# The round count of an expert loop moved from VectorE to GpSimd, and three VectorE instructions reordered in front of the loop

## What is computed

```python
g_logits = z @ w_group + b_group            # 4 groups, the best one is taken
e_logits = z @ w_router + b_router          # 8 experts in each group
top_p, top_i = lax.top_k(softmax(e_in_group), 2)
combine = sum(one_hot(global_idx, 32) * top_w[..., None]) * g_p
for e in range(32):
    gate, up = jnp.split(z @ w_gate_up[e], 2, axis=-1)
    y = y + combine[..., e:e + 1] * ((silu(gate) * up) @ w_down[e])
return rms_norm(x + y, final_norm_g)
```

## Time and profile before

| what | us |
|---|---|
| median of 3 runs | 868.09 |
| lowest and highest run | 867.6, 868.18 |
| span of the profiled execution, first to last instruction | 867.1 |
| start of the first expert step (half 0 on TensorE) | 390.99 |

### The profile page before, as it was taken

How to read it: one execution, slowest core, us unless ns; L and a number is a source line. 1 busy time by engine, 2 the same in 40 slices (tenths; PEclk the granted TensorE clock), 3 DMA queues, 4 the chain that set the end, 5 groups by cost and what they waited for, 6 DMA issues and landing times.

```text
span 867.1 us, 14585 instructions
## 1 busy us (share of the span) xinstructions
PE 852.8 (98%) x5738; PEld 753.9 (87%) x5738; DVE 789.1 (91%) x785; ACT 648.9 (75%) x631; POOL 22.2 (3%) x30
## 2 busy tenths in 40 slices
PE   8999999999999999999999999999999999999996
PEld 6999999999889999877788888888888888888874
DVE  6458999999977787789999999999999999999996
ACT  6563424344554466587999999999999999999996
POOL 0110000000000000016000000000000000000000
PEclk9999999999999999999999999999999999999999
DMA  9952555445452449646999999999999999999971
GB/s 354 425 223 98 193 193 194 178 158 177 169 194 98 144 173 410 248 166 237 392 426 423 429 426 431 428 427 431 427 430 426 430 429 427 430 427 430 426 313 49
DMA packets 20743, 270.70 MB, mean 312 GB/s; under 512 B 2272, under 2 KB 2528, under 8 KB 4448
## 3 DMA queue, kind: packets, MB, share of 16 engines
q1 hardware_dynamic: 20144, 268.33, 75.9%
q10 hardware_dynamic: 560, 1.84, 0.5%
HBM read 269.10 MB, written 1.05 MB: 312 GB/s over the span
## 4 chain that ended last, share of the span: by engine, by line
PE 84%; DVE 13%; issue 2%; ACT 1%; DMA 0%; DVEq 0%; ACTq 0%
PE ps L1598 24%; PE ps L1612 12%; PE ps L1412 9%; PE ps L1414 9%; PE ps L1413 9%; PE ps L1583 4%; PE ps L1622 3%; DVE lo L1117 3%; DVE lo L842 2%; DVE conv L941 2%; PE ps L1429 2%; PE ps L1427 2%; PE ps L1428 2%; PE ps L1696 2%; PE ps L1703 1%
## 5 line engine op out<-in xcount | busy, mean ns | idle before, releaser
L1117 DVE TENSOR_TENSOR lo<-raw,hi 128x2048 fp32r<-128x2048 f32 x142 | 319.1, 2283 | 0.3 <-ACT hi L655 0.3
L655 ACT ACTIVATE hi<-raw 128x2048 fp32r<-128x2048 f32 x141 | 264.9, 1916 | 15.7 <-PE ps L1598 15.7
L444 ACT ACTIVATE hi<-raw 128x2048 fp32r<-128x2048 f32 x62 | 118.6, 1914 | 57.6 <-PE ps L1414 37.6
L842 DVE TENSOR_TENSOR lo<-raw,hi 128x2048 fp32r<-128x2048 f32 x61 | 139.2, 2286 | 20.4 <-ACT hi L444 19.0
L1412 PE MATMUL ps<-inA,hi 128*128 128x256 f32 x544 | 155.0, 285 | 1.4 <-DVE lo L842 1.4
L1598 PE MATMUL ps<-hi,xeT 128*128 128x512 f32 x384 | 154.5, 402 | 0.1
L1414 PE MATMUL ps<-inA,lo 128*128 128x256 f32 x544 | 153.9, 283 | 0.0
L1413 PE MATMUL ps<-inA,hi 128*128 128x256 f32 x544 | 153.9, 283 | 0.0
L1598 PE MATMUL ps<-lo,xeT 128*128 128x512 f32 x384 | 150.2, 391 | 0.0
L1117 DVE TENSOR_TENSOR lo_last<-raw,hi_last 128x2048 fp32r<-128x2048 f32 x48 | 109.6, 2283 | 0.0
L1412 PEld LDWEIGHTS ps<-inA,hi 128*128 128x128 f32 x544 | 104.4, 192 | 2.4 <-DVE lo L842 2.4
(11 more groups left out here) (258 smaller groups left out, 1293.1 us busy)
## 6 DMA issues: line engine op xcount, KB each, us to landing
raw<-in_w_experts SPq DMA_DIRECT2D x96, 2048.0 KB, 13.2
raw<-in_w_dense SPq DMA_DIRECT2D x28, 2048.0 KB, 7.8
raw<-in_w_dense SPq DMA_DIRECT2D x3, 1024.0 KB, 12.6
x_sb<-in_x SPq DMA_DIRECT2D x2, 512.0 KB, 3.6
raw<-in_w_dense SPq DMA_DIRECT2D x2, 512.0 KB, 8.3
mem_sb<-in_mem SPq DMA_DIRECT2D x1, 1024.0 KB, 16.3
x_again<-in_x ACTq DMA_DIRECT2D x1, 1024.0 KB, 17.3
out<-x SPq DMA_DIRECT2D x3, 256.0 KB, 2.1
```

The source lines that it names most:

```text
L444: return nc.scalar.activation(conv_half(hi, N), raw_half(slot, h), ACT.Copy)
L655: nc.scalar.activation(expert_half(hi, N0), raw_flat(slot, k % 2), ACT.Copy).then_inc(hi_made, 1)
L842: nc.vector.tensor_tensor(conv_half(lo, N), raw_half(slot, h), conv_half(hi, N).bitcast(f32), ALU.subtract).then_inc(lo_made, 1)
L1117: nc.vector.tensor_tensor(expert_half(lo, N0), raw_flat(expert_slot(m), k % 2), expert_half(hi, N0).bitcast(f32), ALU.subtract).then_inc(l ...
```

## The change

VectorE keeps the maximum and signals `most_counted` with it. GpSimd compares it and writes `loops`, behind the weights' split and ahead of L423. On VectorE, the low part of half 2 moves ahead of the third piece, `make_pick(1)` and the maximum stand behind the third piece and ahead of the low part of half 3. The waits of the first step on TensorE and ScalarE go to `most_counted`; TensorE waits for `loops_made` before it loads the counts.

```diff
--- before.py
+++ after.py
@@ -219,6 +219,7 @@
         route_for_exp, route_exp, member_made, ranked, rank_made = map(
             sem, ("route_for_exp", "route_exp", "member_made", "ranked", "rank_made"))
         loops_made, comb_made = sem("loops_made"), sem("comb_made")
+        most_counted = sem("most_counted")
         first_again = sem("first_again")
         pick_made, put_made, gathered, xeT_hi, xeT_made = map(sem, ("pick_made", "put_made", "gathered", "xeT_hi", "xeT_made"))
         gate_out, up_out, slotted, slot_sums_made = map(sem, ("gate_out", "up_out", "slotted", "slot_sums_made"))
@@ -419,6 +420,15 @@
             pool_link(nc.gpsimd.tensor_tensor(weight, weight, R["tmp"], ALU.add))
             pool_link(nc.gpsimd.tensor_tensor(total, weight[:, :, 0:PAIRS], weight[:, :, PAIRS:E], ALU.add))
             three_parts(total, lambda k: comb[:, :, :, k], comb_made)
+
+            most, more_turns, further = stat[:, 12:13], stat[:, 13:14], stat[:, 14:15]
+            pool.wait_ge(most_counted, 1)
+            pool_link(nc.gpsimd.tensor_scalar(more_turns, most, float(SLOTS), float(TURNS), ALU.is_gt, ALU.mult))
+            for r in range(2, MAX_ROUNDS):
+                pool_link(nc.gpsimd.tensor_scalar(further, most, float(SLOTS * r), float(TURNS), ALU.is_gt, ALU.mult))
+                pool_link(nc.gpsimd.tensor_tensor(more_turns, more_turns, further, ALU.add))
+            nc.gpsimd.tensor_scalar(loops[:, 1:2], more_turns, float(TURNS - 2), None, ALU.add)
+            nc.gpsimd.tensor_scalar(loops[:, 0:1], more_turns, float(TURNS - 1), None, ALU.add).then_inc(loops_made, 1)
             for r in range(1, MAX_ROUNDS + 1):
                 ins = nc.gpsimd.tensor_scalar(rank_tab[:, :, r * PAIRS:(r + 1) * PAIRS, :], rank_tab[:, :, 0:PAIRS, :],
                                               -float(SLOTS * r), None, ALU.add)
@@ -743,7 +753,7 @@
                 nc.scalar.activation(gu_sb[:, 0:FF], G0, ACT.Copy).then_inc(gate_out, 1)
                 if start:
                     act.wait_ge(comb_made, 2)
-                    act.wait_ge(loops_made, 1)
+                    act.wait_ge(most_counted, 1)
                 else:
                     more(8)
                 if not last_pair:
@@ -1198,7 +1208,6 @@
             nc.vector.reciprocal(w1, w1).then_inc(inverses, 1)
             z_third(1, 0)
             z_third(1, 1)
-            make_pick(1, slice(1, 2))
 
             def first_xeT_lo(piece):
 
@@ -1207,18 +1216,13 @@
                 nc.vector.tensor_tensor(xeT[:, 0, c0:c1, :, SLOTS:2 * SLOTS], first_gathered_view(piece),
                                         xeT[:, 0, c0:c1, :, 0:SLOTS].bitcast(f32), ALU.subtract).then_inc(first_xeT_made, 1)
 
-            for piece in range(3):
-                first_xeT_lo(piece)
+            first_xeT_lo(0)
+            first_xeT_lo(1)
             expert_lo(0, 0, 2)
+            first_xeT_lo(2)
+            make_pick(1, slice(1, 2))
+            nc.vector.tensor_reduce(stat[:, 12:13], ps[:, 5, 2 * PAIRS:3 * PAIRS], AX.X, ALU.max).then_inc(most_counted, 1)
             expert_lo(0, 0, 3)
-            link(nc.vector.tensor_reduce(stat[:, 12:13], ps[:, 5, 2 * PAIRS:3 * PAIRS], AX.X, ALU.max))
-            link(nc.vector.tensor_scalar(stat[:, 13:14], stat[:, 12:13], float(SLOTS), float(TURNS), ALU.is_gt, ALU.mult))
-            for r in range(2, MAX_ROUNDS):
-                link(nc.vector.tensor_scalar(stat[:, 14:15], stat[:, 12:13], float(SLOTS * r), float(TURNS), ALU.is_gt, ALU.mult))
-                link(nc.vector.tensor_tensor(stat[:, 13:14], stat[:, 13:14], stat[:, 14:15], ALU.add))
-            nc.vector.tensor_scalar(loops[:, 1:2], stat[:, 13:14], float(TURNS - 2), None, ALU.add)
-            nc.vector.tensor_scalar(loops[:, 0:1], stat[:, 13:14], float(TURNS - 1), None, ALU.add).then_inc(loops_made, 1)
-
             def slot_weights(i, par):
 
                 dve.wait_ge(put_made, i + 1)
@@ -1664,7 +1668,7 @@
                 if not start:
                     pe.wait_ge(h_made, i)
                 else:
-                    pe.wait_ge(loops_made, 1)
+                    pe.wait_ge(most_counted, 1)
                 gate_or_up(j, at_half, 4, r)
                 if not last_pair:
                     gather(i + 1, (r + 1) % 2, (4, 5, 6, 7))
@@ -1719,6 +1723,7 @@
 
             step(0, 0, slice(0, 1))
             step(0, 1, slice(1, 2))
+            pe.wait_ge(loops_made, 1)
             last_turn = nc.tensor.value_load(loops[0:1, 0:1], min_val=TURNS - 1, max_val=MAX_ROUNDS * TURNS - 1)
             turn_before = nc.tensor.value_load(loops[0:1, 1:2], min_val=TURNS - 2, max_val=MAX_ROUNDS * TURNS - 2)
             with pe.Fori(1, last_turn) as j:
```

## The result

The changed kernel takes 870.56 us (median of 8 runs, 869.67 to 871.89); the kernel before, on the same chip, 868.12 (8 runs, 867.6 to 868.47). The ratio is 1.0029, with a 95% interval of 1.0019 to 1.0038: slower by 2.4 us. The forecast was 869.2 and its range ended at 870.0.

A forecast was written before the change was run, and what follows sets the result against it. VectorE was taken to bound the loop, but its 2.05 us lead to be spent waiting for GpSimd's late comb_made. The delay of +1.15 us made the span 868.3; with 1.0 outside it, 869.2, range 867.1 to 870.0.

The forecast's parts named there:

- What bounds the kernel: Expert loop: VectorE's work fills each 29.16 us step without a gap, so a shift at 429 reaches the end undiminished.
- VectorE's part: Before the second step: seven one-column instructions go and pieces are reordered, so VectorE leads by 2.05 us.
- The count on GpSimd costs nothing: Seven one-column instructions behind the second comb_made take 2 to 15 us, hidden, since nobody needs their result soon.
- Both windows are taken from what stands ahead of the count, one instruction a seam: GpSimd's weight split passes one instruction per low-part seam; comb_made at 405.8, 7.6 us later than now.
- the later, 406.0: Case with GpSimd's L419 caught: comb_made at 406.0, sum +1.4 us; with it through, 405.6 and +1.0.
- The sum of +1.15 for the wait: TensorE and ScalarE wait for comb_made; the delay passes through fold and silu to VectorE's low part: +1.15 us.
- rival 3: TensorE's 2.0 us pause drops the clock to 1.2 GHz for 24 matmuls, 5.7 us more, about 875; chance 0.04.
- Rival 2: Each of five seams costs VectorE a GpSimd instruction's full 0.34 us: +2.8, 870.9; chance 0.07.
- Rival 1: GpSimd in time: more instructions slip in, comb_made by 404.1, VectorE's gain runs on: -0.9, 867.2; chance 0.17.

The follow-up runs named there:

- e3: Changed kernel with the low part of half 2 put back behind the third piece; count stays on GpSimd: 867.41 us, ratio 0.9992.
- e10: The kernel of e3 measured once more: 867.3 us, ratio 0.9992.
- e9: Changed kernel with GpSimd's count moved behind the four rank instructions (L433): 871.57 us (5 runs), ratio 1.0036.
- e5: Changed kernel with ten spare matmuls of 512 columns ahead of TensorE's wait for comb_made: 869.56 us, ratio 1.0019.
- e8: Kernel before, with four more small linked GpSimd instructions ahead of the last split and fourteen spare matmuls in TensorE's wait: 871.07 us, ratio 1.0036.
- e4: Changed kernel without GpSimd's seven weight products ahead of the split (outputs not the reference's), VectorE's program untouched: 867.73 us, ratio 0.9993.
- e6: Kernel before, VectorE untouched, with three more small linked GpSimd instructions ahead of the last split: 868.77 us, ratio 1.0011.
- e7: Kernel before, VectorE untouched, with four more small linked GpSimd instructions ahead of the last split: 872.39 us (5 runs), ratio 1.0060.

## Why the prediction was wrong, point by point

- **What bounds the kernel**: right. The loop's steps take 29.16 us before and after, and what the stretch ahead loses reaches the end.
- **VectorE's part**: right to the hundredth. Low part 4 starts 2.05 us earlier against the mark, and none of it is left at L1186 (the former L1176).
- **The count on GpSimd costs nothing**: right, as far as tenths of a microsecond can be told (e3 and e10, which keep it and lose nothing; e9, where its place makes no difference in the stretch).
- **Both windows are taken from what stands ahead of the count, one instruction a seam**: right. Of the two cases it was the later, 406.0: the forecast's L419 (L420 of the changed kernel) was caught, though by low part 3, since the pick had held the instruction before it. From the mark 18.85 us were forecast for this case and 19.03 measured; the rest fits VectorE's seams, up to 0.07 us each for the 0.02 to 0.04 of the rows. The middle of the two, 405.8, was the value I took, 0.4 too low.
- **The sum of +1.15 for the wait**: the sign and the path were right, the size was short. Where no clock falls, the cost is +1.5 (e5) to +1.8 us (the lower four runs). The forecast had the low part behind silu at 415.1, 27.95 from the mark; with the wait filled it starts 28.47 from it, so 1.65 later than before, half a microsecond more than the sum. The terms that were short are comb_made (0.4) and the way through TensorE's fold and silu (0.1). This alone would have stayed within the range.
- **The step that failed is rival 3, the clock.** The forecast itself put a pause of 2.0 us before TensorE, longer than any in the rows, and yet left the granted clock at full, with 0.04 for the fall. The pause was 2.5 us, and, read from the two groups of times, the clock fell in four of eight runs of the changed kernel and four of five of e9 (one profile of each shows it directly); that it is the pause is shown by e5 and e8. Its price was oversized in turn: all 24 matmuls were charged (+5.7), but eight or nine ran at half clock, so 1.6. Had it stood at 0.5 with +1.6, the range would have reached 869.7 + 1.6 = 871.3 and held the result, and the chance of slower would have been a good half. The sign of being wrong that the forecast named for it, a clock under 1.00 in 400 to 415, is what came.
- **Rival 2** (costly seams) is out: the low parts from 394.99 to 401.80 follow one another in 2.27 us, 0.07 a seam at the most, where 0.12 was the point at which it would decide.
- **Rival 1** gives what the change could have been worth without the starvation: forecast -0.9, measured -0.3 (e4) and -0.7 (e3, e10) in the medians, -0.7 and -0.5 from the mark in the profiles. Most of VectorE's 2.05 us has nowhere to go in either case: the low part of half 2 of the next step needs the high part that ScalarE makes behind silu, silu needs the gate's fold, and that needs TensorE's last half, which VectorE's lead moves little: in e4 the low part waits 0.25 us for that high part again. In the kernel before, that low part started only 0.3 us behind the end of its high part (411.74 + 1.91 = 413.65, against 413.97).

## What to carry to other kernels

An engine's share of busy time (3% for GpSimd) says nothing of how much room it has: here a linked chain of small GpSimd instructions lived between VectorE's low parts, and where such a pause was closed, an instruction took ten times as long (the changed kernel's L417: 0.20 us in the kernel before, 2.22 now). Before taking small instructions or an idle stretch from VectorE, count how many GpSimd instructions pass in it and who waits for the last of them. And where a forecast gives TensorE a pause longer than any that the trace shows with the clock at full, the fall of the clock is a main case and not a remainder.

## What the runs showed of the hardware that was not expected

- Behind one pause of 2.47 us the granted clock went to 1.2 GHz in the profiled execution, and, by the times, in some executions of the same kernel and not in others. With 1.3 us (e6) the profile shows no fall, with 3.6 us (e7) it does, and all five of its runs are above the five of the same kernel with the pause filled. With spare matmuls in the pause the profiles show 2.4 GHz throughout (e5, e8: 1.00 in 400 to 415).
- The pick (two inputs in SBUF, 0.41 us) holds GpSimd as the low parts do: L419 took 0.58 us beside it instead of 0.29. The third piece, which reads one input from PSUM, did not: L418 took 0.29 beside it. The Trainium skill says the same (SBUF — State Buffer, section "Who interferes with whom"): an instruction of VectorE with at most one SBUF input, outside the modes that take two ports, doesn't contend with GpSimd; one with two contends with a GpSimd instruction that reads SBUF. The rule that the prediction took from the section "SBUF: two separate sides", that the one who starts first holds the pair for the whole instruction, is seen here for VectorE's instructions only: a GpSimd instruction at a seam cost VectorE 0.02 to 0.07 us, and not the 0.2 to 0.3 that it takes by itself.
